# Cross-attention's output tiles in another order, the activations' sums made beside them, and fourteen pairs of tiles in each MLP

## The reference, cut to what matters

```python
h = h + mixer(...)
h = h + cross_attention(rms_norm(h, norm_xattn_g[l]), mem_n, wq[l], wkv[l], wo[l])
h = h + sq_relu_mlp(rms_norm(h, norm_mlp_g[l]), mlp_w1[l], mlp_w2[l])

def cross_attention(h, mem_n, wq, wkv, wo):      # 4 heads of 256, 256 memory rows
    ...
    return o @ wo                                 # 1024 x 1024

def sq_relu_mlp(h, w1, w2):                       # 1024 -> 4096 -> 1024
    a = relu(h @ w1)
    return (a * a) @ w2
```

## Time and profile before

| | |
|---|---|
| median of three runs | 2213.02 us |
| the profiled execution | 2213.02 us |
| its span, first to last instruction | 2211.1 us |
| TensorE busy | 2196.4 us, 99% |
| VectorE busy | 1452.8 us, 66% |
| ScalarE busy | 977.1 us, 44% |
| bytes read from HBM | 235.37 MB |

### The profile page before, as it was taken

One profiled execution on the slowest core, in us unless ns is written; L12 is line 12 of the kernel. 1 busy time (PEld: TensorE's weight loads), 2 busy tenths in 40 slices (PEclk: granted clock), 3 DMA queues, 4 the chain that ended last, 5 costly groups with the idle time before them and its releaser, 6 DMA issues.

```text
span 2211.1 us, 31738 instructions
## 1 busy us (share of the span) xinstructions
PE 2196.4 (99%) x12112; PEld 1860.6 (84%) x12112; DVE 1452.8 (66%) x2444; ACT 977.1 (44%) x1680; POOL 14.5 (1%) x14
## 2 busy tenths in 40 slices
PE   9999999999999999999999999999999999999998
PEld 7887888888778888888898888998888888899997
DVE  5866665558656566686665767766755657776775
ACT  5444543434445244475554544443322435444444
POOL 0000000000000000200000000000000000000000
PEclk9999999999999999999999999999999999999999
DMA  5555443245644323464353233333332213233331
GB/s 202 178 180 162 152 122 109 96 132 181 179 142 153 115 96 119 124 190 143 110 166 125 86 106 101 99 104 97 96 95 96 86 48 105 95 97 104 96 110 54
DMA packets 136695, 268.14 MB, mean 121 GB/s; under 512 B 21774, under 2 KB 79932, under 8 KB 136161
## 3 DMA queue, kind: packets, MB, share of 16 engines
q1 hardware_dynamic: 136544, 266.13, 38.9%
HBM read 235.37 MB, written 26.77 MB: 119 GB/s over the span
## 4 chain that ended last, share of the span: by engine, by line
PE 96%; DVE 2%; DMA 1%; ACT 1%; POOL 1%; issue 0%; SPq 0%; DVEq 0%; POOLq 0%; ACTq 0%
PE ps L2119 30%; PE ps L2121 30%; PE ps L2120 29%; PE ps L2147 2%; PE ps L2136 2%; POOL t_UP L2102 1%; DMA far<-t_UP 0%; PE ps L2171 0%; PE ps L2161 0%; PE ps L2159 0%; PE ps L2160 0%; PE ps L2173 0%; PE ps L2172 0%; PE ps L2190 0%; DVE t_Tb L2666 0%
## 5 line engine op out<-in xcount | busy, mean ns | idle before, releaser
L2119 PE MATMUL ps<-t_P0H,t_whi 128*128 128x512 f32 (+1 forms) x1568 | 590.8, 377 | 2.8 <-DVE t_P0L L2483 1.7
L2120 PE MATMUL ps<-t_P0L,t_whi 128*128 128x512 f32 (+1 forms) x1568 | 584.6, 373 | 0.0
L2121 PE MATMUL ps<-t_P0H,t_wlo 128*128 128x512 f32 (+1 forms) x1464 | 553.0, 378 | 0.0
L2438 DVE TENSOR_TENSOR t_wlo<-t_raw,t_whi 128x1024 fp32r<-128x1024 f32 (+2 forms) x289 | 342.2, 1184 | 48.4 <-PE ps L2121 36.2
L2262 ACT ACTIVATE t_whi<-t_raw 128x1024 fp32r<-128x1024 f32 (+2 forms) x295 | 300.6, 1024 | 155.0 <-PE ps L2121 153.4
L2119 PEld LDWEIGHTS ps<-t_P0H,t_whi 128*128 128x128 f32 x1568 | 295.4, 188 | 72.1 <-issue 15.5
L2120 PEld LDWEIGHTS ps<-t_P0L,t_whi 128*128 128x128 f32 x1568 | 295.1, 188 | 56.1 <-issue 1.0
L2121 PEld LDWEIGHTS ps<-t_P0H,t_wlo 128*128 128x128 f32 x1464 | 275.3, 188 | 54.7
L2119 PE MATMUL ps<-t_P1H,t_whi 128*128 128x512 f32 (+1 forms) x548 | 210.1, 383 | 1.6 <-DVE t_P1L L2821 1.0
L2120 PE MATMUL ps<-t_P1L,t_whi 128*128 128x512 f32 (+1 forms) x548 | 208.5, 380 | 0.0
L2121 PE MATMUL ps<-t_P1H,t_wlo 128*128 128x512 f32 (+1 forms) x524 | 201.1, 384 | 0.0
(11 more groups left out here) (348 smaller groups left out, 3877.7 us busy)
## 6 DMA issues: line engine op xcount, KB each, us to landing
t_raw<-in_wts SPq DMA_DIRECT2D x362, 512.0 KB, 3.6
far<-t_Tb SPq DMA_DIRECT2D x26, 384.0 KB, 3.1
far<-t_Tb SPq DMA_DIRECT2D x16, 512.0 KB, 3.7
t_PTX<-far SPq DMA_DIRECT2D x64, 96.0 KB, 3.4
t_raw<-in_wts SPq DMA_DIRECT2D x16, 384.0 KB, 3.1
t_QKV<-far SPq DMA_DIRECT2D x32, 128.0 KB, 3.0
t_raw<-in_wts SPq DMA_DIRECT2D x13, 256.0 KB, 2.9
t_PTX<-far SPq DMA_DIRECT2D x24, 128.0 KB, 2.7
```

The source lines that it names most:

```text
L2119: e.matmul(s.out, s.sh, s.mh, start=s.first, stop=False, skip_group_check=again)
L2120: e.matmul(s.out, s.sh, s.ml, start=False, stop=False, skip_group_check=again)
L2121: i = e.matmul(s.out, s.sl, s.mh, start=False, stop=s.end, skip_group_check=again)
L2438: e.tensor_tensor(s.dst, s.raw, s.hi.bitcast(F32), ALU.subtract).then_inc(*mark("lo", s.j))
```

## The change

The output tiles of cross-attention run in the order 0, 4, 1, 5, 2, 6, 3, 7, and most of the combines are issued behind them. The MLP has four first tiles instead of eight, and fourteen pairs, n = 0 to 13. The first two pairs have two second-stage tiles each (at i = 1 and 3) and one chunk of second-stage weights each; at i = 0 and 2 `other` issues nothing.

```diff
+        order = (0, 4, 1, 5, 2, 6, 3, 7)
+        steps = {2: ["gain 0"], 3: ["add 0"], 4: ["high 0", "gain 1"], 5: ["low 0", "add 1"], 6: ["high 1", "gain 2"],
+                 7: ["low 1", "add 2"]}
...
-            for m in range(2):
+            for m in order[:2]:
                 open_.append(wo(m))
...
         if open_:
-            open_.append(wo(2))
+            open_.append(wo(order[2]))
             for _ in range(6):
                 next(open_[2])
-        for g in open_:
-            run(g)
-        for m in range(len(open_), 8):
-            run(wo(m))
-            if m == 5:
-                combine("gain 0", "gain 1")
-            elif m == 6:
-                combine("add 0")
+        for n in range(8):
+            run(open_[n] if n < len(open_) else wo(order[n]))
+            combine(*steps.get(n, []))
         row_end()
...
-        w0 = [Weight(chunk("mlp_w1", l, halves(0), halves(128 * i, 1))) for i in range(8)]
-        w20 = [Weight(chunk("mlp_w2", l, halves(0, 4), halves(256 * i, 2))) for i in range(2)]
+        w0 = [Weight(chunk("mlp_w1", l, halves(0), halves(128 * i, 1))) for i in range(4)]
         raws = {}
-        for n in range(2, 14):
+        for n in range(14):
             cols, c, m = 512 + 256 * n, (n - 1) // 2, 4 * ((n - 1) % 2)
             raws[n] = [own(chunk("mlp_w1", l, halves(0), halves(cols + 128 * i, 1))) for i in range(2)]
-            raws[n] += [own(chunk("mlp_w2", l, halves(512 * c, 4), halves(128 * m + 256 * i, 2))) for i in range(2)]
+            if n < 2:
+                raws[n] += [own(chunk("mlp_w2", l, halves(0, 4), halves(256 * n, 2)))]
+            else:
+                raws[n] += [own(chunk("mlp_w2", l, halves(512 * c, 4), halves(128 * m + 256 * i, 2))) for i in range(2)]
...
         def w2(n, k):
-            if not dry:
+            if not dry and 2 + k < len(raws[n]):
...
+        combine("high 2", "gain 3")
         run(first_tile(0, w0[0]))
-        combine("high 0")
+        combine("low 2", "add 3")
         run(first_tile(1, w0[1]))
-        combine("low 0", "add 1")
+        combine("high 3")
+        u0(0)
         run(first_tile(2, w0[2]))
-        combine("high 1", "gain 2")
+        combine("low 3")
+        low(0, "u0")
+        sums(0)
+        u1(0)
         run(first_tile(3, w0[3]))
...
+        low(0, "u1", 0)
+        u2(0)
+        w2(0, 0)
+        low(0, "u2", 1)
+        u3(0)
...
             def other(i):
-                run(second_tile(c2, m2 + i, u[f"w{i // 2}"], i % 2))
+                if n >= 2:
+                    run(second_tile(c2, m2 + i, u[f"w{i // 2}"], i % 2))
+                elif i % 2:
+                    run(second_tile(0, 2 * n + i // 2, u["w0"], i // 2))
                 return "mm", tiles[0] - 1
...
             c11 = add(a0, z, s1, p)
             PB.give(bz, c11)
+            if n == 0:
+                flush()
             other(0)
-            if n == 2:
-                low(n, "w1", 3)
...
-        for n in range(2, 14):
+        for n in range(0, 14):
```

More of the change, by code:

```diff
@@ L1769, in sums @@
                 s = emit("sums", t=S1, a11=raw_of(i, 0, 512), a12=raw_of(i, 512, 512), a21=raw_of(j, 0, 512),
-                         a22=raw_of(j, 512, 512), need=[landed(j), U[n]["u0"].key] + (tfree if n == 2 else []))
+                         a22=raw_of(j, 512, 512), need=[landed(j), U[n]["u0"].key] + (tfree if n == 0 else []))
                 U[n]["sums"] = s.id
@@ L1855, in pair_of_tiles @@
             s1 = snap(a0, p, af)
-            if n == 2:
+            if n == 0:
                 low(n, "u3")
                 low(n, "w0", 2)
-                w2(n, 1)
             else:
```

## The result

The kernel after the change takes 2227.18 us, the median of five runs (2225.88 to 2228.05), beside 2213.07 for five runs of the kernel before: ratio 1.0062, 95% interval 1.0048 to 1.0076. It is slower, 1.3 us above the forecast. The profiled execution took 2228.05, its span 2226.3 (before 2211.1).

What follows compares the result with a forecast made beforehand. TensorE's matmul issue, 99% busy, was taken to bound the kernel. Waits of 8.9 us a layer, 17.8 in two, less 4.9 of matmul gain, put 12.9 on 2213.02: forecast 2225.9 us, range 2217 to 2233.

Steps and rivals of the forecast that it cites:

- Matmul gain: Both MLPs: two pairs replace four first-stage tiles, 2.35 us less a layer, 4.9 in all with cheaper second-stage matmuls.
- The row of squares: Behind the first MLP tile: TensorE waits for VectorE's later split of the squares, 1.3 us lost a layer.
- Up to the first pair: First four MLP tiles: TensorE ends the fourth at 24.0 us from the first tile's start, with u0 in time.
- T2 of the first pair: First pair's third product waits for the first product's snapshot behind ScalarE's queue, starting at 30.25: 3.5 us lost a layer.
- B22 of the first pair: First pair's product directly behind T1 on the same bank waits for a queued snapshot: 1.7 us lost a layer.
- T2 and B22 of the second pair: Second pair's snapshot waits: 1.6 us lost without tile cover, then 0.8 for a bare turn-around, a layer.
- Rival A: First pair of each layer: TensorE's clock falls, costing 1.75 us a layer (2229.4) or twice as long (2232.9); chance 0.26.
- The forecast's own sign against itself: Stretches of the forecast waits: a granted clock below 1.00 there would show the forecast wrong.
- B: Seam: squares and snapshots reached earlier than queued, half the loss above bare turn-arounds goes; 2218.6 us, chance 0.13.
- C: ScalarE reaches the first pair's snapshot by 26.85, only four bare turn-arounds are paid; not slower, 2211.3 us, chance 0.08.
- D: First two pairs: turn-arounds hidden too, the full gain of 4.9 us stays; 2208.1 us, chance 0.03.
- The lower bound in the prediction: First two pairs: four bare turn-arounds of 0.8 us, 3.2, as the least the change adds.

Runs made afterwards that it cites:

- e4: Kernel before with only the new cross-attention output-tile order and the combines behind them, eight first tiles kept; 2215.74 us, ratio 1.0008.
- e7: Changed kernel with six first tiles and thirteen pairs, each with four second-stage tiles, and sums issued later; 2210.86 us, ratio 0.9988.
- e1: Changed kernel plus 24 unused 256-column matmuls in the first pair, between the second product and the third; 2225.65 us, ratio 1.0056.
- e2: Changed kernel with the second-stage tiles moved to i = 1 and 2 in the first pair, 0 and 2 in the second; 2222.5 us, ratio 1.0045.
- e3: Changed kernel with the moved second-stage tiles of e2 and the 24 unused matmuls of e1; 2219.11 us, ratio 1.0027.
- e5: Changed kernel with low 1, add 2, high 2 and gain 3 issued behind the split of the sum of squares; 2229.39 us, ratio 1.007.
- e6: Changed kernel without the norms' division: a multiply-add writing a constant replaces the reciprocals on VectorE; 2226.19 us, ratio 1.0053.
- e8: Changed kernel with the first pair's splits u2, w and u3 issued behind the first product's snapshot instead of ahead; 2229.38 us, ratio 1.0069.

## Why the prediction was right, and where its steps were not

T to pair n = 2, in us. "Queued" is a sum of queues for the first layer: 56.1 + 8.9 - 2.45 = 62.55 for the kernel after, and for the others this (62.6), or 56.1 for e4 and e7, with the change that their expectation names. "Both seams" and "time" are what the kernel has more than the kernel before, the time by the medians of one chip.

| kernel | queued | first layer | second layer | clock fell | both seams | time |
|---|---|---|---|---|---|---|
| before | | 56.09 | 56.29 | no | | |
| after | 62.6 | 63.00 | 63.09 | both | 13.7 | 14.1 |
| e1 filler | 62.6 | 62.70 | 62.55 | no | 12.9 | 12.0 |
| e2 cover moved | 58.7 | 60.10 | 60.36 | both | 8.1 | 8.9 |
| e3 both | 58.7 | 58.83 | 58.83 | no | 5.3 | 5.5 |
| e4 cross-attention only | 57.4 | 57.39 | 57.63 | no | 2.6 | 1.5 |
| e5 sums late | 63.5 | 65.10 | 64.75 | both | 17.5 | 15.2 |
| e6 no division | 62.0 | 62.48 | 62.12 | first | 12.2 | 12.0 |
| e7 thirteen pairs | 54.9 | 55.02 | 54.81 | no | -2.6 | -2.8 |
| e8 snapshot first | 62.9 | 64.39 | 64.41 | both | 16.4 | 15.2 |

Where the clock stays up in the first layer, the queues are within about 0.1 us of the trace. Where it falls, 0.4 to 1.6 come on top. Of these sums only that of the kernel after was on record before the result.

**Matmul gain, right.** e7's first seam keeps 1.07 of a counted 1.17 (the second gains 1.48), and the sum of the first layer closes with 2.45.

**The row of squares, right.** 1.23 and the restart, forecast 1.3; e4 isolates it.

**Up to the first pair, right.** It began at T + 24.03, forecast 24.0, with no wait for u0.

**T2 of the first pair, right.** 3.45 and the restart against 3.5. e6 and e8 show how far each queue holds it: with 2.9 less of VectorE's work T2 comes 0.6 earlier, because VectorE then waits for TensorE's third tile; with three of ScalarE's passes out of the way its wait is 1.04.

**B22 of the first pair, wrong in the kernel as made.** 1.7 was forecast, 0.63 + 0.11 came. The snapshot's queue had the length that I gave it: with a full clock (e1, and e6's second layer) the wait is 1.75 to 1.76. What the step left out is that T1, on which the snapshot also depends, is late when T2 and T3 run at half clock. Of the 1.4 lost there in the first layer, 1.1 was taken out of this wait (1.76 in e1, 0.63 here), and the seam was 0.4 above the queue.

**T2 and B22 of the second pair, right.** 1.49 and 0.63, each plus 0.11, against 1.6 and 0.8.

**The clock.** Rival A named the place and the cause, and its event happened in both layers; I gave it 0.26 and its price was 1.75 or 3.5 a layer. The forecast's own sign against itself, a granted clock below 1.00 in those stretches, came true, so the number held and the path to it did not in full. The event's own cost was 1.4 and 1.6, which the price of 1.75 nearly meets; the step of rival A that failed is that it was added to the sum. It is a delay of TensorE ahead of a wait, and the wait shrinks by it. The forecast came close partly because these two errors, B22 too long and the clock left out, nearly cancel. They are tied to each other, as e1 shows, but the prediction didn't foresee it, so this closeness is luck. The profiled execution is 2.15 above the forecast (the median 1.3). Of this 0.8 is the seams' (6.9 and 6.8 measured for the queued 6.45 twice), and the rest lies at the program's start and end, for which the prediction has no term.

**Rivals B, C and D** are out. Both T2 waits were as long as queued, the snapshot ahead of the first ended at T + 30.3 and not by 26.85, and no turn-around was hidden; only the two B22 paid the bare one. The lower bound in the prediction was itself too small: 3.2 is four bare turn-arounds, those of one layer, and two layers have eight, 6.4. With it B would have been 2220.2, and C 2214.5 instead of 2211.3, above the kernel before. A wait on a DMA at the seam did not turn up at all.

The cause of the slowdown in one sentence: the first two pairs must save their block product between accumulations on one bank while VectorE and ScalarE still make their operands, and the four second-stage tiles that exist by then stand at none of the four places, before T2 and before B22, where a snapshot is waited for. Placed there (e2) they cover three of the four in full or nearly, but the wait of the first T2 and that of the squares stay, and the kernel is still slower than before. A gain of 4.9 met waits of 16 and 3.0 of half clock. What stays open is why the clock fell with a wait of 2.86 us in one layer of e6 and not with 2.90 in the other.

## What to carry to other kernels

Count the cover before you extend a scheme with fewer products: each snapshot or turn-around on one bank needs independent matmuls beside it, and when the supply of those is used up, the next unit costs more than it saves; here thirteen pairs gain and fourteen lose, in each order of tiles that was tried. An engine's average (ScalarE 44%) says nothing on a seam, while a queue written down pass by pass was good to about 0.1 us as long as the clock stayed up. A loss on the engine in front of another wait is not to be added to it: take the later of the two.

## What the hardware did that I had not expected

A single long wait in the middle of otherwise full work was enough for half clock. In the seams of these nine kernels it came with waits of 3.4 to 3.5 us (four of four: after and e2), of 5.0 (two of two, e5) and of 2.9 (three of four: e8 twice, where it was the last of four waits in the pair, and e6's first layer, but not its second), and with none of 1.8 or less. It did not come at a fixed moment of the wait: between 1.8 us ahead of the wait's end (e5's second layer) and 1.2 behind it (the second layer of the kernel after). The lower level lasted 3.41 us, and 6.83 in e5. A fall of 3.41 us cost TensorE 1.4 to 1.6 us in matmuls of mostly 256 columns, and 24 matmuls that compute nothing kept the clock up in e1 and e3.

Restart and turn-around are steady: a matmul behind a semaphore wait is followed by the next about 0.11 us late, and a product that stands directly behind its predecessor on the same bank, with the snapshot in between, loses 0.63 + 0.11 = 0.74 at least, in both pairs and both layers.
